# The operands of all 256-column matmuls move to rows of 1024 bytes, at 128 modulo 256

## The reference, cut to what matters

```
h = h + hgrn2_mix(h)              # 4 x 2048 columns in, gated linear recurrence, 2048 out
k, v, F = fox_shared_kv(h)        # keys, values, forget sums for all 272 tokens
h = h + fox_mix(h, k, v, F)       # q and z: (norm(h) * g) @ w_in, attention, @ w_out
x = h[16:]                        # from here on 256 tokens
x = x + mixed(x) @ w_out          # convolution and sliding-window attention, mixed
x = x + peer(norm(x))             # expert layer: u (16384 x 2048), top-k gates, v
```

## The kernel before, in words

| tensor | starts at | modulo 256 | one row is |
|---|---|---|---|
| `whi` (weights, rounded) | 57,856 | 0 | 512 bytes for the 128 columns of one `kk` |
| `wlo` (weights, low part) | 24,416 | 96 | 512 bytes for one `kk` |
| `xb_hi`, `xb_lo` | 91,648 and 109,056 | 0 | 1088 bytes (272 columns) |
| `xa_hi`, `xa_lo` | 126,464 and 143,872 | 0 | 1088 bytes |
| `e_coef_hi` | 22,240 | 224 | 1024 bytes, one row per buffer |
| `e_coef_lo` | 144,128 | 0 | 1024 bytes, one row per buffer |
| `e_coef_first` (the first tile of each down part alone) | 228,096 | 0 | 1024 bytes |

## Time and profile before

### The profile page before, as it was taken

How to read it: one execution, slowest core, us unless ns; L and a number is a source line. 1 busy time by engine, 2 the same in 40 slices (tenths; PEclk the granted TensorE clock), 3 DMA queues, 4 the chain that set the end, 5 groups by cost and what they waited for, 6 DMA issues and landing times.

```text
span 3040.3 us, 63437 instructions
## 1 busy us (share of the span) xinstructions
PE 3000.6 (99%) x25230; PEld 2943.4 (97%) x25230; DVE 1947.1 (64%) x3277; ACT 1616.5 (53%) x2611; POOL 665.5 (22%) x293
## 2 busy tenths in 40 slices
PE   9999998999999999989999999999999999999999
PEld 8999998999999998869999999999999999999999
DVE  6777776644544568758777798554458865555544
ACT  6777675566788643455444444444444444444443
POOL 3333333444444432115444300000000000000000
PEclk9999999999999999989999999999999999999999
DMA  5444443544444454325555544555554455555554
GB/s 207 151 152 149 141 152 132 176 166 166 167 139 150 146 180 153 113 78 196 173 187 182 180 148 159 182 192 186 187 193 155 153 189 184 190 183 193 181 192 166
DMA packets 72432, 506.67 MB, mean 167 GB/s; under 512 B 7920, under 2 KB 10480, under 8 KB 11504
## 3 DMA queue, kind: packets, MB, share of 16 engines
q1 hardware_dynamic: 71728, 503.16, 48.4%
q10 hardware_dynamic: 576, 1.72, 0.2%
HBM read 502.75 MB, written 2.10 MB: 166 GB/s over the span
## 4 chain that ended last, share of the span: by engine, by line
PE 95%; DVE 3%; ACT 2%; issue 0%; DMA 0%; SPq 0%; DVEq 0%; ACTq 0%
PE bank L451 12%; PE bank L450 12%; PE bank L452 12%; PE bank L464 6%; PE bank L2312 4%; PE banks L2312 4%; PE bank L2313 4%; PE banks L2313 4%; PE bank L2314 4%; PE banks L2314 4%; PE bank L2085 3%; PE bank L2086 3%; PE bank L2087 3%; PE banks L2085 3%; PE banks L2086 3%; PE banks L2087 3%
## 5 line engine op out<-in xcount | busy, mean ns | idle before, releaser
L427 ACT ACTIVATE whi<-raw 128x1024 fp32r<-128x1024 f32 x896 | 941.8, 1058 | 988.5 <-PE bank L452 366.1
L434 DVE TENSOR_TENSOR wlo<-raw,whi 128x1024 fp32r<-128x1024 f32 x667 | 851.4, 1287 | 429.2 <-ACT whi L427 428.2
L434 POOL TENSOR_TENSOR wlo<-raw,whi 128x1024 fp32r<-128x1024 f32 x231 | 608.4, 2634 | 937.0 <-ACT whi L427 925.8
L450 PE MATMUL bank<-xa_hi,whi 128*128 128x272 f32 (+1 forms) x1984 | 576.0, 290 | 4.2 <-DVE wlo L434 4.1
L451 PE MATMUL bank<-xa_lo,whi 128*128 128x272 f32 (+1 forms) x1984 | 567.5, 286 | 0.0
L452 PE MATMUL bank<-xa_hi,wlo 128*128 128x272 f32 (+1 forms) x1984 | 566.5, 286 | 0.0
L450 PEld LDWEIGHTS bank<-xa_hi,whi 128*128 128x128 f32 x1984 | 372.8, 188 | 6.7 <-issue 5.1
L451 PEld LDWEIGHTS bank<-xa_lo,whi 128*128 128x128 f32 x1984 | 374.1, 189 | 1.3
L452 PEld LDWEIGHTS bank<-xa_hi,wlo 128*128 128x128 f32 x1984 | 372.9, 188 | 0.0
L450 PE MATMUL bank<-xb_hi,whi 128*128 128x256 f32 (+1 forms) x1120 | 317.9, 284 | 1.5 <-DVE wlo L434 1.5
L451 PE MATMUL bank<-xb_lo,whi 128*128 128x256 f32 (+1 forms) x1120 | 316.4, 283 | 0.0
(11 more groups left out here) (458 smaller groups left out, 6787.9 us busy)
## 6 DMA issues: line engine op xcount, KB each, us to landing
raw<-in_w SPq DMA_DIRECT2D x250, 1024.0 KB, 4.8
raw<-in_v SPq DMA_DIRECT2D x128, 1024.0 KB, 5.3
raw<-in_u SPq DMA_DIRECT2D x96, 1024.0 KB, 4.9
hT<-in_hT SPq DMA_DIRECT2D x4, 544.0 KB, 6.9
out<-hT SPq DMA_DIRECT2D x8, 256.0 KB, 2.4
raw<-in_w SPq DMA_DIRECT2D x2, 512.0 KB, 6.1
r_keys<-in_keys ACTq DMA_DIRECT2D x1, 1024.0 KB, 4.9
c_mask<-in_masks ACTq DMA_DIRECT2D x1, 320.0 KB, 3.0
```

The lines of the kernel that those rows point to most:

```text
L427: act.activation(whi[:, (2 * t.q + half) % 4, :], raw[:, t.q, half * 1024:(half + 1) * 1024], ACT.Copy).then_inc(w_hi_done, 1)
L434: eng.tensor_tensor(wlo[:, t.q, at], raw[:, t.q, at], whi[:, slot, :].bitcast(F32), ALU.subtract).then_inc(w_lo_done[half], 1)
L450: te.matmul(ps, hi, x[0][:, kk, cols], start=(kk == 0), stop=False)
```

## The change

New tensors `yb` and `ya`, each a pair of hi and lo with rows of 256 columns (1024 bytes), take the same places as `xb` and `xa`, each behind a gap of 32 floats (128 bytes). Every stage with 256 columns writes and reads them; stages with 272 columns keep `xb` and `xa`. Worked out from the addresses above, `yb_hi` starts at 91,776, `yb_lo` at 109,184, `ya_hi` at 126,592 and `ya_lo` at 144,000: all four are at 128 modulo 256, in every row. The fill of `yb` in the key and value stage writes 256 columns in place of 272. No tensor behind them moves, since a `y` tensor with its gap (16,512 bytes) is smaller than the `x` tensor that shares its place (17,408). The numbers of instructions, waits and DMAs stay.

```diff
+SQUARE_GAP = {"hi": 32, "lo": 32}
...
-        xb = (tensor(ctx, "xb_hi", [P, KT, L], F32R), tensor(ctx, "xb_lo", [P, KT, L], F32R))
+
+        def rows_of(name, part):
+
+            with ExitStack() as st:
+                tensor(st, f"{name}_{part}_gap", [P, SQUARE_GAP[part]])
+                return tensor(st, f"{name}_{part}", [P, KT, SEQ], F32R)
+
+        yb_hi = rows_of("yb", "hi")
+        xb_hi = tensor(ctx, "xb_hi", [P, KT, L], F32R)
+        yb = (yb_hi, rows_of("yb", "lo"))
+        xb = (xb_hi, tensor(ctx, "xb_lo", [P, KT, L], F32R))
...
+        ya_hi = rows_of("ya", "hi")
+        xa_hi = tensor(innermost, "xa_hi", [P, KT, L], F32R)
+        ya = (ya_hi, rows_of("ya", "lo"))
+        xa = (xa_hi, tensor(innermost, "xa_lo", [P, KT, L], F32R))
...
-        OUT = ((T_AOUT, xb, cols_all, "kv_norm", xa, 1), (T_BOUT, xa, cols_q, "norm1", xn1, 3),
-               (T_WOUT, xa, cols_q, "norm2", xb, 4))
+        OUT = ((T_AOUT, xb, cols_all, "kv_norm", xa, 1), (T_BOUT, ya, cols_q, "norm1", xn1, 3),
+               (T_WOUT, ya, cols_q, "norm2", yb, 4))
...
-                        act.activation(at3(xb[0], h), at3(hT, h), ACT.Copy, scale=par("b_norm", h))\
+                        act.activation(at3(yb[0], h), at3(hT, h, cols_q), ACT.Copy, scale=par("b_norm", h))\
...
-                        project(te, Tile(T_QZ, i, 2 * u), xb, cols_q)
+                        project(te, Tile(T_QZ, i, 2 * u), yb, slice(0, SEQ))
...
-                    te.matmul(ps, hi, xb[0][:, kk, 0:SEQ], start=(kk == 0), stop=False)
-                    te.matmul(ps, hi, xb[1][:, kk, 0:SEQ], start=False, stop=False)
-                    last = te.matmul(ps, lo, xb[0][:, kk, 0:SEQ], start=False, stop=(kk == KT - 1))
+                    te.matmul(ps, hi, yb[0][:, kk, :], start=(kk == 0), stop=False)
+                    te.matmul(ps, hi, yb[1][:, kk, :], start=False, stop=False)
+                    last = te.matmul(ps, lo, yb[0][:, kk, :], start=False, stop=(kk == KT - 1))
```

More of the change, by code:

```diff
@@ L489, in out_piece @@
         def out_piece(te, base, tile, kks):
-            x, n = (xb, L) if base == T_AOUT else (xa, SEQ)
+            x, n = (xb, L) if base == T_AOUT else (ya, SEQ)
             t = Tile(base, 0, tile)
@@ L1030, in body @@
                         ve.wait_ge(x_hi_done, SPLITS[T_KV] + h + 1)
-                        ve.scalar_tensor_tensor(at3(xb[1], h), at3(hT, h), par("b_norm", h),
-                                                at3(xb[0], h).bitcast(F32), ALU.mult, ALU.subtract)\
+                        ve.scalar_tensor_tensor(at3(yb[1], h), at3(hT, h, cols_q), par("b_norm", h),
+                                                at3(yb[0], h).bitcast(F32), ALU.mult, ALU.subtract)\
                             .then_inc(x_split, 1)
@@ L1128, in body @@
                     if within(h, HEADS):
-                        project(te, Tile(T_QZ, i, 2 * u + 1), xb, cols_q)
+                        project(te, Tile(T_QZ, i, 2 * u + 1), yb, slice(0, SEQ))
                         te.wait_ge(qsq_done, h + 1)
@@ L1253, in body @@
                         ve.wait_ge(x_hi_done, SPLITS[T_QZ] + h - 1)
-                        ve.tensor_tensor(at3(xa[1], h - 2, slice(0, SEQ)), one3(f.mm[:]),
-                                         at3(xa[0], h - 2, slice(0, SEQ)).bitcast(F32), ALU.subtract)\
+                        ve.tensor_tensor(at3(ya[1], h - 2), one3(f.mm[:]),
+                                         at3(ya[0], h - 2).bitcast(F32), ALU.subtract)\
                             .then_inc(x_split, 1)
@@ L1466, in wout_piece @@
                 hi, lo = whi[:, slot, k * P:(k + 1) * P], wlo[:, t.q, kk * P:(kk + 1) * P]
-                te.matmul(ps, hi, xa[0][:, kk, 0:SEQ], start=(kk == 8), stop=False)
-                te.matmul(ps, hi, xa[1][:, kk, 0:SEQ], start=False, stop=False)
-                last = te.matmul(ps, lo, xa[0][:, kk, 0:SEQ], start=False, stop=(kk == KT - 1))
+                te.matmul(ps, hi, ya[0][:, kk, :], start=(kk == 8), stop=False)
+                te.matmul(ps, hi, ya[1][:, kk, :], start=False, stop=False)
+                last = te.matmul(ps, lo, ya[0][:, kk, :], start=False, stop=(kk == KT - 1))
             if k0 == KT - 2:
@@ L1661, in lo_conv @@
                 ve.wait_ge(x_hi_done, x_count("conv", k))
-                ve.tensor_tensor(xa[1][:, k:k + 2, 0:SEQ], c.cv[:, k:k + 2, :],
-                                 xa[0][:, k:k + 2, 0:SEQ].bitcast(F32), ALU.subtract).then_inc(x_split, 2)
+                ve.tensor_tensor(ya[1][:, k:k + 2, :], c.cv[:, k:k + 2, :],
+                                 ya[0][:, k:k + 2, :].bitcast(F32), ALU.subtract).then_inc(x_split, 2)
             def conv_gated(k):
@@ L1822, in body @@
                     if static(i) and i + s == 0:
-                        project(te, t, xb, slice(0, SEQ), skipped=2, ps=route_ps(t.q), halves=(0,))
+                        project(te, t, yb, slice(0, SEQ), skipped=2, ps=route_ps(t.q), halves=(0,))
                         out_sum(te, T_WOUT, SEQ)
-                        project(te, t, xb, slice(0, SEQ), skipped=2, ps=route_ps(t.q), halves=(1,))
+                        project(te, t, yb, slice(0, SEQ), skipped=2, ps=route_ps(t.q), halves=(1,))
                     else:
-                        project(te, t, xb, slice(0, SEQ), skipped=2, ps=route_ps(t.q))
+                        project(te, t, yb, slice(0, SEQ), skipped=2, ps=route_ps(t.q))
                     if p - 1 in KEY_AT:
```

9 lines of the change are left out of this document (4 added, 5 removed).

## The result

The changed kernel takes 3061.46 us (median of six runs, 3059.54 to 3063.47); the kernel before, beside it, 3040.20 (six runs, 3039.73 to 3043.2). The ratio is 1.0065, with a 95% interval of 1.0055 to 1.0075: 21.3 us slower. I had forecast 12 us faster.

The account below looks back on a forecast made before the run. PE, 99% busy with matmuls without gaps, bounds the kernel: their number times their pitch. From 3042.1 us, 3.7 ns times 3328 triples, 12.3 us, comes off, giving 3029.8, stated as 3030; range 3016 to 3044.

Parts of the forecast that it names:

- What bounds the kernel, and how much moves: Whole kernel: PE's gapless matmuls, busy 99%, set the time; 3328 triples with 256 columns move from `x` to `y`.
- Everything else stays: Down part stays at 116.2 ns per matmul, HGRN as it was; 272-column stages keep their places.
- The smaller fill: Key and value stage: VectorE writes 256 columns, not 272; hidden, so zero, or 2.5 us gain if uncovered.
- Even spacing, no period of four: QZ and up part: first members start evenly, 0.348 us apart on average, without the four-row pattern.
- The price of the triple: Moved stages: 112.5 + 116.7 + 118.8 = 348.0 ns against 351.7, a gain of 3.7 ns per triple.
- a direct row: 112.5: First member, `hi` at 128 with next weights at 0: 112.5 ns, read from the up part's row at offset 128.
- a first member that was cheap only because the member before it had run long: Listed sign of error in the moved triples: 112.5 ns might depend on the 120.0 ahead of it; no size given.
- a disturbance of about 1 ns: QZ and unrolled parts of the up stage run at about 353 ns, not 351.7; left as it is.
- Slower: Rival, moved stages: a bad relation of third and first member repeats every triple, 356.7 ns, loss 16.6 us, 3059; chance 0.08.
- the turning point: Moved triples: the change turns slower where the third member exceeds 122.5 ns.
- Deeper gain: Rival, moved stages: third member near 114 to 115 as in down part, triple 344.5, gain 24 us, 3018; chance 0.14.
- The rule of the Trainium skill: Activations' place wouldn't matter to matmuls, so the change brings nothing; 0.03 for this within the no-change rival, 3040 to 3045.

Follow-up runs that it names:

- t3: Changed kernel with a separate fixed (hi, lo) place modulo 256 per stage: QZ (96, 224), outputs (128, 224) and (160, 224), router and up (128, 64); 3047.22 us.
- s1: Changed kernel with a separate fixed (hi, lo) place per stage: QZ (0, 0), outputs (224, 0) and (0, 128), router and up (128, 0); 3058.44 us.
- s3: Changed kernel with a separate fixed (hi, lo) place per stage: QZ (96, 96), outputs (160, 160) and (224, 224), router and up (64, 0); 3056.92 us.
- v3: Changed kernel with a tiny bf16 matmul after every fourth triple of the looped second up part, and a wait for `flushed` ahead of it; 3080.89 us.
- u4: Changed kernel with fixed places per stage, `whi` and everything behind it 64 bytes lower, `wlo` unmoved; 3065.29 us.
- u1: Changed kernel with `lo` of both pairs at 64 modulo 256, `hi` still at 128; 3040.20 us, ratio 0.9995 to the kernel before.
- v2: u2 with `xa`, read by 272-column stages, in rows of 1280 bytes at (128, 64); 3025.20 us, ratio 0.9943 to the kernel before.
- u2: u1 with the down part's pair also moved to (128, 64); 3022.33 us, ratio 0.9938 to the kernel before.
- s2: Changed kernel with a separate fixed (hi, lo) place per stage: QZ (64, 64), outputs (192, 192) and (32, 32), router and up (224, 0); 3054.13 us.

## Why the prediction was wrong

**What bounds the kernel, and how much moves: right.** PE is still 99% busy, its wait on `wlo` is 5.3 us, no engine is late. One reading was off, without effect: the prediction puts every other engine at 209 of 279 us or less in three stages, 75%, but ScalarE's 197 of 249 in QZ is 79%. 3328 triples times the change of their prices gives the whole difference (22.3 us against 21.3).

**Everything else stays: right.** Down part 348.9, HGRN's 272-column triples 375.6, as said. The smaller fill brought nothing that shows.

**Even spacing, no period of four: right in form, wrong in size.** 360.0 ns, not 348.

**The price of the triple: the step that failed.** I put 112.5 + 116.7 + 118.8 together from rows of the trace of before. The third, the one I had no row for and bounded with care, was not the trouble: it runs at 116.6, even cheaper. The first, which had "a direct row: 112.5", runs at 123.4, and the second at 120.0 rather than 116.7. The row for the first was direct in its place only. In the trace of before, the 112.5 follows a third member of 120.0, in a pattern of four rows. With all rows at 128 that pattern is gone, and the cheap member with it. Whether the long member ahead makes the next one cheap isn't shown: in t3 every first member takes 113.4 behind a third of 117.6. What is shown is that 112.5 isn't a steady price at (128, 128). I had written this down among the things that would make me wrong, "a first member that was cheap only because the member before it had run long", and gave it no rival and no price, so the range didn't reach it.

The trace of before had a sign of this. The prediction left aside "a disturbance of about 1 ns" in QZ and in the first tiles of the up parts. It is two rhythms at the same places: from one QZ tile to the next the triples take 351.7 and 354.0 by turns (the seventh to fourteenth behind each break), and in the second up part 352.6 and 353.4, until the last 700 or so, which nothing interrupts, take 351.7. A price that changes at a break, with no place modulo 256 changed, doesn't belong to the place alone.

The changed kernel's own trace shows the passage. This is its timeline in the router, behind a break by the key products (L1848); only the first members are shown:

```profile
1477.91 0.60 PE L1848 MATMUL banks<-r_keys,r_qT 128*128 128x128 f32 x4
1478.27 0.36 PE L464 MATMUL banks<-yb_hi,whi 128*128 128x256 f32 x1
...
1478.71 0.28 PE L464 MATMUL banks<-yb_hi,whi 128*128 128x256 f32 x1
...
1479.07 0.27 PE L464 MATMUL banks<-yb_hi,whi 128*128 128x256 f32 x1
...
1479.41 0.28 PE L464 MATMUL banks<-yb_hi,whi 128*128 128x256 f32 x1
...
1479.76 0.28 PE L464 MATMUL banks<-yb_hi,whi 128*128 128x256 f32 x1
...
1480.11 0.28 PE L464 MATMUL banks<-yb_hi,whi 128*128 128x256 f32 x1
...
1480.47 0.29 PE L464 MATMUL banks<-yb_hi,whi 128*128 128x256 f32 x1
...
1480.83 0.29 PE L464 MATMUL banks<-yb_hi,whi 128*128 128x256 f32 x1
```

Differences of the starts: 0.44 (the restart), 0.36, 0.34, 0.35, 0.35, 0.36, 0.36. Over the 16 such breaks of the router stage the restarted triple takes 439.2 and those behind it 360.8, 346.6, 348.4, 349.2, 358.2 and then 360.0 as long as nothing interrupts. Member by member, from the third triple on, first + second + third: 112.4 + 116.8 + 117.4, 113.4 + 117.4 + 117.6, 118.3 + 113.3 + 117.6, 121.6 + 120.0 + 116.6, 123.4 + 120.0 + 116.6. The first of these triples follows a third member of 120.0. It is, to 0.1 ns in every member, the row class that I had taken for a steady price, and it is a passing state.

**The rivals.** "Slower" gave 3059 and 3061 came, but by half of its mechanism. One price does repeat in every triple. It isn't the third member over 122.5, where I had put the turning point (it is 116.6), but the first at 123.4 and the second at 120.0. The sum landed because the earlier trace rows, the only triple with `hi` and `lo` at one fixed place that I had, is of a dear kind too; it is another pair, (0, 0), so that 3059 came so near is in part luck. That row alone was the best evidence on the page for this change, and it got a chance of 0.08. "Deeper gain" leaned on the earlier trace rows, a fixed place at 348.9; s1 to s3 and v3 show that the same places also run at 355.6.

**The rule of the Trainium skill** (TensorE: Matmul & The Clock Gate, Part 2: loading the next weights "doesn't steal SBUF read bandwidth from the running matmul") would, as the prediction reads it, have made every place equal. The runs contradict that result, though they don't show by what port or path: moving `lo` alone by 64 bytes takes a settled triple from 360.0 to 346.7 (after, t3), and moving `whi` and the activations 64 bytes against `wlo` takes the up part's (128, 64) from 347.0 to 359.5 (u4).

**What stays open.** Why (128, 64) is cheap and (128, 128) dear, and which of its two rhythms a pair takes at an entry, was not found. Only the times are shown, not what collides. The outputs ran at 353.4 in u1 (the first) and v2 and at 347 in u2, with equal places modulo 256, and a stretch of u2's own first up segment ran at 353.3. So the next edit may lose u2's good rhythm again. The four runs of u2 span 2.9 us, so its down part kept its rhythm in all of them; nothing is known of shorter stretches.

## What to carry to other kernels

When matmuls run without gaps, read the price of a place only from a stretch in which every operation has that same place for many triples; a price cut out of a mixed pattern belongs to its neighbours as well. Before laying out anything anew, spend a run on the candidates, one pair of places per stage, since the settled prices reach from 346.7 to 360.0 ns and no average or nearness foretold them. Look at each unbroken stretch by itself, since a mean over a stage can hide two prices, as in s2 and in the QZ stage of before. Compare the untouched stages too: a gain of 15.1 us in the moved stages of u1 was given back by one that nobody had touched.

## What was unexpected of the hardware

The pitch of a 256-column fp32r matmul at granted clock 1.00 goes from 115.6 (346.7 / 3) to 120.0 ns (360.0 / 3), depending on the places of weights and activations modulo 256.

At (128, 128), behind a break in the router, the restarted triple and five more pass (2.2 us) before the triple takes 360.0, and that holds until the next break. The triple right behind the tiny matmul takes 75 ns more than a settled one (435.0 against 360.0, v3).

Equal code at equal places settles at either of two prices: (224, 0) at 348.9 or 355.6, (128, 64) at 346.7 or 353.4. In s2 the two change at breaks in a regular order, and the triple with the break in it tells which comes: 436 or 437 ns ahead of a dear stretch of the router, 443 or 444 ahead of a cheap one.
